# Loading the expert stage's tables and weights in 1 MB pieces, four slots in flight instead of two of 2 MB

## The chip, the core and the metric

The kernel runs on one core of a Trainium2 chip. The core has TensorE (PE in the profile; PEld is its weight load), VectorE (DVE), ScalarE (ACT), GpSimd (POOL) and SyncE (SP), each with its own instruction stream, 16 DMA engines that they share. Of the tiles named below, `bank` is PSUM and all others are SBUF. All data is float32. The metric is the device time of one execution in microseconds (us); lower is better.

## The reference

One inference step of a two-layer backbone over 640 tokens (128 context, 512 latent; five blocks of 128) of width 1024. Each layer has a mixer (retention and Fourier mixing in layer 0, a convolution module in layer 1) and then the expert stage that this change is about. Every sub-layer is shifted, scaled and gated by rows that come from the conditioning vectors through a 1024 x 6144 matrix per layer (`ada_w`). The expert stage, cut to what is computed:

```
q = (x @ w_q).reshape(T, PEER_HEADS, 2, PEER_DQH)
scores = jnp.einsum('thsd,hskd->thsk', q, sub_keys)
s, i = lax.top_k(scores, PEER_TOPK)
cand = s[:, :, 0, :, None] + s[:, :, 1, None, :]          # 16 x 16 sums per head
cidx = i[:, :, 0, :, None] * PEER_NKEYS + i[:, :, 1, None, :]
top, sel = lax.top_k(cand, PEER_TOPK)
idx = jnp.take_along_axis(cidx, sel, axis=-1)             # 8 heads x 16 experts of 16384
g = jax.nn.softmax(top, axis=-1)
a = jax.nn.gelu(jnp.einsum('td,thkd->thk', xb, u_tab[ib]))
out = jnp.einsum('thk,thkd->td', g * a, v_tab[ib])
```

`w_q` is 1024 x 2048, and `u_tab` and `v_tab` have 16384 rows of 1024, 64 MB each per layer.

## The kernel before

The expert stage (`peer` in each engine's block) splits the tokens. For the first two blocks (GB = 2) the chosen rows are gathered: GpSimd issues 256 indirect DMAs of u rows and 256 of v rows per layer, 512 KB each, into rings of four, and VectorE does one dot product instruction per u gather (`dot`, L1336) and one multiply-add per v gather (`add`, L1354). For the other three blocks (DB = 3, 384 tokens) all 16384 experts are computed on TensorE: the tables are streamed from HBM, the activations of all experts are taken with gelu, and a dense gate matrix, zero where an expert was not chosen, is multiplied in.

The stage has two halves. In the **first half** TensorE works through jobs. `peer_jobs` (L375) lists them: 16 `q` jobs (128 columns of w_q against 640 tokens), 128 `u` jobs (128 experts against 384 tokens; 4 of them are a chunk of the table), and, in layer 0 only, 12 `ada` jobs (512 columns of layer 1's `ada_w` against the two conditioning vectors), one behind every second u chunk. Each job ends in one ScalarE instruction (`take_job`, L1009) that empties its bank of PSUM, and `job(n)` (L700) starts only when job n-2 is taken. The jobs' operands come in loads of 2 MB: four q jobs, four u jobs or one ada job share one. There are two slots, `load_slot` (L221), and SyncE (`peer_weights`, L486) issues load n into the slot of load n-2 when the last job of load n-2 is done. Between these it writes the finished activations of a chunk (768 KB, `acts`, L498) and the ada row (4 KB, `mod_rows`, L501) to HBM, and before it can write either, it waits until ScalarE has taken the job. SyncE's queue is in order. ScalarE's take of ada row i waits until the write of row i-1 has landed (`ada2_out`), since both use the same 512 columns of `ada_raw`.

Between the jobs TensorE also does the scores of the queries against the keys (`score`, L721; 40 per layer), which VectorE turns into the top 16 (`choose`, L1255), and, when all picks are made, 96 scatters per layer (`scatter`, L742) that make the dense gates out of one-hot rows which VectorE writes (`hot`, L1357, L1366 and L1368). VectorE's order is written out by `dve_order` (L393): dots and adds alternate at a steady pace with the choose, batch and hot steps between them. The stretch with the hot steps is called the **hot part** below, and what lies ahead of it in the first half the **choosing part**. `peer_steps_of` (L423) is a planner: it estimates when VectorE will want each score and scatter and puts them between the jobs by a table of costs, `COST = {"q": 8.9, "u": 5.4, "ada": 7.1}` us. ScalarE follows the same list.

The **second half** starts when the last job is taken, the last scatter is taken and the gates have been written to HBM. It streams v_tab, gates and activations through other slots and ends the stage. Of it the change touches only that two of its three v slots are described without `load_slot`; they are the same bytes.

Of the kernel before, what the change touches and what calls it, by code (L numbers as in the profile page):

```python
# [9 lines left out]
ALU = mybir.AluOpType  # L10
# [116 lines left out]
def program(nc, x_in, cond_t, norm_gain, final_gain, ada_w, ada_b, ada_fix_in, ab_w_in, ab_w_out, decays, states,  # L127
# [3 lines left out]
    with ctx:  # L131
# [89 lines left out]
        load_slot = [ring[:, i * 4096:(i + 1) * 4096] for i in range(2)]  # L221
# [9 lines left out]
        v_slot = [t.rearrange("p (j d) -> p j d", j=CT) for t in (work[:, 5120:9216], *load_slot)]  # L231
# [70 lines left out]
        load_in = per_stage("load_in", 2)  # L302
# [3 lines left out]
        top_ready = per_stage("top_ready", LAYERS); exp_ready = per_stage("exp_ready", LAYERS)  # L306
        idx_ready = per_stage("idx_ready", LAYERS)
        ijg_ready = sem("ijg_ready"); oh_ready = per_stage("oh_ready", LAYERS)
# [3 lines left out]
        gelu_ready = per_stage("gelu_ready", LAYERS)  # L312
# [4 lines left out]
        v_done = per_stage("v_done", LAYERS); d_sums = per_stage("d_sums", LAYERS)  # L317
# [12 lines left out]
        def chunk(parts, s, done, after=None):  # L330
# [7 lines left out]
                for c in range(8)]  # L338
# [6 lines left out]
                       ((u_free[0], ROWS), (v_free[0], ROWS), (d_sums[0], DB), (d_sums[0], DB))[c]) for c in range(4)]  # L345
# [29 lines left out]
        def peer_jobs(l):  # L375

            loads, jobs = [], []
            for c in range(CHUNKS):
                if c in (0, 2, 6, 10):
                    q = (0, 2, 6, 10).index(c)  # L380
                    loads.append(("q", q, len(jobs) + 4))
                    jobs += [("q", 4 * q + i, len(loads) - 1) for i in range(4)]
                loads.append(("u", c, len(jobs) + CT))
                jobs += [("u", c * CT + i, len(loads) - 1) for i in range(CT)]
                if l == 0 and c % 2 and c // 2 < ADA:
                    loads.append(("ada", c // 2, len(jobs) + 1))
                    jobs.append(("ada", c // 2, len(loads) - 1))
            return loads, jobs
# [32 lines left out]
        COST = {"q": 8.9, "u": 5.4, "ada": 7.1}  # L421
# [42 lines left out]
        load_base = [(0, 0), tuple(16 * ((len(plans[0][0]) + 1 - i) // 2) for i in range(2))]  # L464
# [19 lines left out]
        def _(sp):  # L484

            def peer_weights(l):  # L486
# [3 lines left out]
                for n in range(len(loads) + 2):  # L490
                    if n < 2:
                        sp.wait_ge(*first[n])
                    else:
                        kind, i, end = loads[n - 2]
# [7 lines left out]
                    if n == len(loads) or n == len(loads) + 1:  # L502
                        continue
# [1167 lines left out]
```

## Time and profile before

| | us |
|---|---|
| median of three runs | 4314.09 |
| lowest, highest | 4311.28, 4319.12 |
| the profiled execution, whole | 4313.75 |
| its span on the core | 4311.9 |
| mean granted TensorE clock | 0.965 of full speed |
| busy: PE / DVE / POOL / ACT | 4059.6 / 2616.0 / 1440.1 / 473.0 |
| moved by DMA | 1128.44 MB, 262 GB/s on average |

A row of the profile names a line of the kernel, an engine, an operation, and what it writes and reads (`ring<-in_peer_ut` is a load of the u table into the ring; `bank<-hT,ring` are the q and u jobs, `bank<-ring,stat` the ada jobs, `bank<-bc` the scatters; `bc` at L1366 and L1368 the hot steps). Idle time stands before the instruction that ended it, with the thing that released it. Many helper calls share one line: all matmuls are at L652, all ScalarE instructions at L952, so the names tell them apart. Of the mean granted clock, 1.0 is 2.4 GHz and 0.5 is 1.2 GHz. The DMA share is the mean busy share of the 16 DMA engines.

### The profile page before, as it was taken

To read this page: it belongs to the slowest core of one execution; us is meant where nothing else is said; L and a number is where in the kernel's file an instruction comes from. 1 tells how busy PE (TensorE), PEld (TensorE's weight loads), DVE (VectorE), ACT (ScalarE), POOL (GpSimd) and SP (SyncE) were. 2 spreads that over 40 slices of the span, in tenths; PEclk is the share of its full clock that TensorE was granted. 3 is DMA by queue.
4 is the path that set the end of the run, shared out by engine and by line. 5 is a ranking of instruction groups with operands and counts; after the bars stand their busy time and mean duration, and the time that the engine had idled before them with its cause. 6 is when DMAs were issued, how large, how long until landed. Compare 5 with 4: busy or idle time off the path is not lost.

```text
span 4311.9 us, 35262 instructions
## 1 busy us (share of the span) xinstructions
PE 4059.6 (94%) x12920; PEld 2247.2 (52%) x12920; DVE 2616.0 (61%) x5488; ACT 473.0 (11%) x879; POOL 1440.1 (33%) x1072
## 2 busy tenths in 40 slices
PE   8997899989999998999998999999999986999998
PEld 1655555555555663444444545666656664444443
DVE  2303577767767884433434954888887887443444
ACT  2010111101111220000001121111112221000000
POOL 0000014444445553333320000454555565333331
PEclk9998999999999998999999999999999986999999
DMA  8111247778889999888873100788889999888875
GB/s 318 60 58 62 93 171 288 282 269 314 313 314 348 355 343 374 318 331 322 316 281 123 59 30 20 280 313 298 328 330 342 353 330 321 356 328 321 321 304 184
DMA packets 349757, 1128.44 MB, mean 262 GB/s; under 512 B 23424, under 2 KB 139632, under 8 KB 328712
## 3 DMA queue, kind: packets, MB, share of 16 engines
q0 software_dynamic: 153632, 560.15, 35.2%
q1 hardware_dynamic: 96880, 515.69, 31.0%
q10 hardware_dynamic: 99072, 50.33, 3.9%
q8 instruction: 103, 1.69, 0.2%
q14 instruction: 70, 0.57, 0.0%
HBM read 1025.01 MB, written 101.07 MB: 261 GB/s over the span
## 4 chain that ended last, share of the span: by engine, by line
PE 88%; DMA 6%; DVE 5%; ACT 1%; issue 0%; SPq 0%; ACTq 0%; POOL 0%; DVEq 0%
PE bank L652 88%; DMA ring<-in_peer_ut 2%; DMA peer_gates<-work 2%; DMA ring<-in_peer_w_q 1%; DVE bc L1366 1%; DVE diag L1354 1%; DVE ring L1336 1%; DVE bc L1368 1%; DMA ring<-in_ada_w 1%; ACT work L952 0%; ACT hT L952 0%; DMA bc<-peer_gates 0%; DVE work L1190 0%; DVE work L1192 0%; PE bank L696 0%
## 5 line engine op out<-in xcount | busy, mean ns | idle before, releaser
L652 PE MATMUL bank<-hT,ring 128*128 128x384 f32 (+3 forms) x5696 | 1808.5, 477 | 59.5 <-DMA ring<-in_peer_ut 30.3
L652 PEld LDWEIGHTS bank<-hT,ring 128*128 128x128 f32 x5696 | 1062.0, 193 | 728.0 <-issue 89.2
L612 POOL DMA_INDIRECT ring<-in_peer_u,work x512 | 769.9, 1504 | 1728.4 <-DVE ring L1336 1456.6
L652 PE MATMUL bank<-ring,work 128*128 128x512 f32 x2016 | 868.8, 592 | 0.0
L612 POOL DMA_INDIRECT ring<-in_peer_v,work x512 | 644.5, 1259 | 302.1 <-issue 155.6
L1354 DVE SCALAR_TENSOR_TENSOR diag<-ring,work,diag 128x1024 f32<-128x1024 f32 x508 | 652.8, 1285 | 29.5 <-DMA ring<-in_peer_v,work 26.1
L1336 DVE SCALAR_TENSOR_TENSOR ring<-ring,work 128x1024 f32<-128x1024 f32 x512 | 622.2, 1215 | 22.7 <-DMA ring<-in_peer_u,work 22.7
L652 PEld LDWEIGHTS bank<-ring,work 128*128 128x128 f32 x2016 | 383.0, 190 | 482.2 <-issue 482.2
L1393 DVE TENSOR_TENSOR work<-work,bc 128x1536 f32<-128x1536 f32 x64 | 112.4, 1758 | 717.2 <-PE bank L652 666.0
L952 ACT ACTIVATE work<-bank 128x384 f32<-128x384 f32 (+3 forms) x540 | 290.7, 541 | 2029.8 <-PE bank L652 1928.6
L652 PE MATMUL bank<-work 128*128 128x512 f32 x1056 | 461.3, 597 | 30.8 <-DVE work L1393 30.8
L652 PE MATMUL bank<-ring,hT 128*128 128x384 f32 (+1 forms) x960 | 351.0, 524 | 8.5 <-ACT hT L952 8.5
L652 PEld LDWEIGHTS bank<-work 128*128 128x128 f32 x1056 | 202.2, 192 | 285.5 <-issue 285.5
L1366 DVE TENSOR_SCALAR bc<-keep,bc 128x128 f32<-128x128 f32 x768 | 214.0, 363 | 132.6 <-PE bank L652 82.8
L652 PE MATMUL bank<-bc 128*128 128x128 f32 x1536 | 225.1, 304 | 61.8 <-DVE bc L1368 58.6
L652 PEld LDWEIGHTS bank<-ring,hT 128*128 128x128 f32 x960 | 180.9, 191 | 162.4 <-issue 73.4
L652 PEld LDWEIGHTS bank<-bc 128*128 128x128 f32 x1536 | 215.0, 215 | 96.7 <-DVE bc L1368 67.1
L652 PE MATMUL bank<-ring,stat 128*2 128x512 f32 x384 | 168.5, 596 | 16.6 <-DMA ring<-in_ada_w 16.6
L1263 DVE MAX8 small<-bank 128x8 f32<-128x128 f32 x160 | 39.8, 290 | 222.6 <-PE bank L652 221.8
L1588 DVE SCALAR_TENSOR_TENSOR work<-work,small 128x670 f32<-128x670 f32 x180 | 149.5, 918 | 0.0
L952 ACT ACTIVATE work<-work 128x16 f32<-128x16 f32 (+3 forms) x49 | 14.1, 303 | 1164.1 <-DVE ring L1336 1151.2
L1368 DVE TENSOR_TENSOR bc<-bc,keep 128x512 f32<-128x512 f32 x192 | 132.1, 688 | 0.0
(156 smaller groups left out, 1595.1 us busy)
## 6 DMA issues: line engine op xcount, KB each, us to landing
ring<-in_peer_ut SPq DMA_DIRECT2D x64, 2048.0 KB
ring<-in_peer_vt SPq DMA_DIRECT2D x42, 2048.0 KB, 7.9
ring<-in_ada_w SPq DMA_DIRECT2D x24, 2048.0 KB, 14.4
peer_gates<-work ACTq DMA_DIRECT2D x48, 1024.0 KB
bc<-peer_gates SPq DMA_DIRECT2D x32, 1536.0 KB
peer_acts<-work SPq DMA_DIRECT2D x60, 768.0 KB
work<-peer_acts SPq DMA_DIRECT2D x60, 768.0 KB, 15.1
work<-in_peer_vt SPq DMA_DIRECT2D x22, 2048.0 KB, 7.9
```

The lines of the kernel that those rows point to most:

```text
L612: nc.gpsimd.indirect_dma_start(row, None, table, bass.IndirectOffsetOnAxis(ap=idx_all[:, i:i + 1], axis=0)).then_inc(s, 16)
L652: return nc.tensor.matmul(out, lhsT, rhs, start=start, stop=stop, **kw)
L952: return nc.scalar.activation(out, in_, func, **kw)
L1263: own.mark(v.max(side_v[:, s, 0:8], sc[s]))
L1336: v.scalar_tensor_tensor(out=row, in0=row, scalar=1.0, in1=h_tok[:, n % GB, :], op0=ALU.mult, op1=ALU.mult, accum_out=dots[:, n % 2, k:k + ...
L1354: v.scalar_tensor_tensor(out=a, in0=row, scalar=wgt[:, n % 2, k:k + 1], in1=a, op0=ALU.mult, op1=ALU.add).then_inc(v_free[l], 1)
L1366: v.tensor_scalar(oh[:, n % 2, 0, o, :], iota, ijg_t[:, 0, t0 + o:t0 + o + 1], ijg_t[:, 2, t0 + o:t0 + o + 1], ALU.is_equal, ALU.mult)
L1368: v.tensor_tensor(oh[:, n % 2, 1, :, :], ijg_t[:, 1, t0:t0 + OH].unsqueeze(2).to_broadcast([P, OH, NKEYS]), iota.unsqueeze(1).to_broadcast ...
L1393: v.tensor_tensor(w, a, g, ALU.mult).then_inc(w_ready[l], 1)
L1588: ins = v.scalar_tensor_tensor(out=y_conv[:, f, :], in0=src, scalar=w, in1=y_conv[:, f, :], op0=ALU.mult, op1=ALU.add)
```

## The change

The same bytes are loaded in pieces of half the size into four slots. A q load or a u load now feeds two jobs. An ada load is 256 columns, so one ada job becomes two of half the width: 24 jobs, 24 takes and 24 writes of 2 KB. Load n goes into the slot of load n-4 when that load's last job is done. The write of a u chunk stays whole, behind the second half of a chunk. Loads in layer 0: 96 instead of 48; in layer 1: 72 instead of 36. The rows of w_q and ada_w that a load reads are 1 KB long instead of 2 KB, those of u_tab 8 KB instead of 16 KB. The planner gets `"ada": 3.6` for the half job. Six pairs of per-layer semaphores (`top_ready`, `exp_ready`, `idx_ready`, `oh_ready`, `gelu_ready`, `d_sums`) become one counter each that goes on counting in layer 1.

```
-        load_slot = [ring[:, i * 4096:(i + 1) * 4096] for i in range(2)]
+        load_slot = [ring[:, i * 2048:(i + 1) * 2048] for i in range(4)]
...
+            def load_of(kind, c, n):
+                loads.append((kind, c, len(jobs) + n))
+                jobs.extend((kind, c * n + i, len(loads) - 1) for i in range(n))
+
             for c in range(CHUNKS):
-                if c in (0, 2, 6, 10):
-                    q = (0, 2, 6, 10).index(c)
-                    loads.append(("q", q, len(jobs) + 4))
-                    jobs += [("q", 4 * q + i, len(loads) - 1) for i in range(4)]
-                loads.append(("u", c, len(jobs) + CT))
-                jobs += [("u", c * CT + i, len(loads) - 1) for i in range(CT)]
+                for q in [n for n, at in enumerate((0, 0, 2, 2, 6, 6, 10, 10)) if at == c]:
+                    load_of("q", q, 2)
+                for half in range(2):
+                    load_of("u", 2 * c + half, 2)
                 if l == 0 and c % 2 and c // 2 < ADA:
-                    loads.append(("ada", c // 2, len(jobs) + 1))
-                    jobs.append(("ada", c // 2, len(loads) - 1))
+                    for half in range(2):
+                        load_of("ada", c // 2 * 2 + half, 1)
...
-        COST = {"q": 8.9, "u": 5.4, "ada": 7.1}
+        COST = {"q": 8.9, "u": 5.4, "ada": 3.6}
...
-                for n in range(len(loads) + 2):
-                    if n < 2:
-                        sp.wait_ge(*first[n])
+                for n in range(len(loads) + 4):
+                    if n < 4:
+                        if n % 2 == 0:
+                            sp.wait_ge(*first[n // 2])
                     else:
-                        kind, i, end = loads[n - 2]
+                        kind, i, end = loads[n - 4]
                         sp.wait_ge(jobs_done[l], end)
-                        if kind == "u" and i < CHUNKS - KEPT:
+                        if kind == "u" and i % 2 and i // 2 < CHUNKS - KEPT:
                             sp.wait_ge(job_taken[l], end)
-                            sp.dma_start(acts[l, i], a_stage[i % 2]).then_inc(a_out[i % 2], 16)
+                            sp.dma_start(acts[l, i // 2], a_stage[i // 2 % 2]).then_inc(a_out[i // 2 % 2], 16)
                         if kind == "ada":
                             sp.wait_ge(job_taken[l], end)
-                            sp.dma_start(mod_rows[1][:, i * CH:(i + 1) * CH], ada_raw).then_inc(ada2_out, 16)
...
+                            sp.dma_start(mod_rows[1][:, i * 256:(i + 1) * 256], ada_raw[:, 0:256]).then_inc(ada2_out, 16)
...
-                        pe.wait_ge(load_in[ld % 2], load_base[l][ld % 2] + 16 * (ld // 2 + 1))
+                        pe.wait_ge(load_in[ld % 4], load_base[l][ld % 4] + 16 * (ld // 4 + 1))
...
                     elif kind == "ada":
                         if i:
                             act.wait_ge(ada2_out, 16 * i)
-                        f(ada_raw, bank[0:2, 2 * (n % 2), :]).then_inc(job_taken[l], 1)
+                        f(ada_raw[:, 0:256], bank[0:2, 2 * (n % 2), 0:256]).then_inc(job_taken[l], 1)
```

Two places show what moves. The first is SyncE's queue in layer 0, from the load of the second ada piece to that of the third, at a point where no q load follows. `peer_acts<-work` writes a finished u chunk, `mod_rows<-work` an ada row. Before:

```order
L508 DMA ring<-in_ada_w 128x8x512
L498 DMA peer_acts<-work 128x1536 [waits job_taken0,jobs_done0]
L506 DMA ring<-in_peer_ut 128x4096
L501 DMA mod_rows<-work 2x512 [waits job_taken0,jobs_done0]
L506 DMA ring<-in_peer_ut 128x4096
L498 DMA peer_acts<-work 128x1536 [waits job_taken0,jobs_done0]
L508 DMA ring<-in_ada_w 128x8x512
```

And now:

```order
L512 DMA ring<-in_ada_w 128x8x256 [waits jobs_done0]
L502 DMA peer_acts<-work 128x1536 [waits job_taken0,jobs_done0]
L512 DMA ring<-in_ada_w 128x8x256
L510 DMA ring<-in_peer_ut 128x2048 [waits jobs_done0]
L502 DMA peer_acts<-work 128x1536 [waits job_taken0,jobs_done0]
L510 DMA ring<-in_peer_ut 128x2048
L505 DMA mod_rows<-work 2x256 [waits job_taken0,jobs_done0]
L510 DMA ring<-in_peer_ut 128x2048
L505 DMA mod_rows<-work 2x256 [waits job_taken0,jobs_done0]
L510 DMA ring<-in_peer_ut 128x2048
L512 DMA ring<-in_ada_w 128x8x256 [waits jobs_done0]
```

Before, the u load that TensorE needs right behind the ada job is issued behind the write of the u chunk just ahead of that job. Now the first half of that table chunk stands two jobs earlier, ahead of the write, and only its second half stands behind it. There are two writes of ada rows, each with its own wait for ScalarE.

The second place is ScalarE's queue in layer 0 around the fourth and fifth ada rows; 128x384 are the takes of u jobs, 128x640 of q jobs, `small<-small 128x80` is the exponential of the softmax for which VectorE waits. Before:

```order
L952 ACTIVATE work<-bank 2x512 [waits ada2_out,jobs_done0]
L952 ACTIVATE work<-bank 128x384 [waits a_out0,jobs_done0]
L952 ACTIVATE work<-bank 128x384 [waits jobs_done0] x3
L952 ACTIVATE work<-bank 128x384 [waits a_out1,jobs_done0]
L952 ACTIVATE work<-bank 128x384 [waits jobs_done0] x3
L952 ACTIVATE work<-bank 2x512 [waits ada2_out,jobs_done0]
L952 ACT_TABLE_LOAD
L952 ACTIVATE small<-small 128x80 [waits top_ready0]
L952 ACTIVATE work<-bank 128x640 [waits scores0,jobs_done0] x4
```

And now:

```order
L956 ACTIVATE work<-bank 2x256 [waits ada2_out,jobs_done0] x2
L956 ACTIVATE work<-bank 128x384 [waits a_out0,jobs_done0]
L956 ACTIVATE work<-bank 128x384 [waits jobs_done0] x3
L956 ACTIVATE work<-bank 128x384 [waits a_out1,jobs_done0]
L956 ACTIVATE work<-bank 128x384 [waits jobs_done0] x3
L956 ACTIVATE work<-bank 2x256 [waits ada2_out,jobs_done0]
L956 ACT_TABLE_LOAD
L956 ACTIVATE small<-small 128x80 [waits top_ready]
L956 ACTIVATE work<-bank 2x256 [waits ada2_out,jobs_done0]
L956 ACTIVATE work<-bank 128x640 [waits scores0,jobs_done0] x4
```

Each take of an ada row waits for the write of the row before it. Before, eight takes of u jobs (and more) lie between two of them; now every second one stands directly behind the take whose write it waits for, or with the exponential between them.

## Rows read from the trace of the kernel before

**Rows 1.** The page, chain that ended last, by engine.
```profile
PE 88%; DMA 6%; DVE 5%; ACT 1%; issue 0%; SPq 0%; ACTq 0%; POOL 0%; DVEq 0%
```

**Rows 2.** Waits of PE, layer 0, choosing part: total us, times, longest.
```profile
PE bank L652 <- DMA ring<-in_peer_ut: 26.0, 6, 5.4
PE bank L652 <- DMA ring<-in_peer_w_q: 25.9, 3, 10.5
```

**Rows 3.** PE by form, layer 0 choosing part: count, busy, mean ns, idle before.
```profile
L652 PE MATMUL bank<-hT,ring 128*128 128x384 f32 x1153 | 389.5, 499 | 26.0 <-DMA ring<-in_peer_ut 26.0
L652 PE MATMUL bank<-hT,ring 128*128 128x320 f32 x384 | 110.6, 449 | 25.9 <-DMA ring<-in_peer_w_q 25.9
```

**Rows 4.** The same of layer 1, choosing part.
```profile
L652 PE MATMUL bank<-hT,ring 128*128 128x384 f32 x1344 | 438.4, 486 | 0.0
L652 PE MATMUL bank<-hT,ring 128*128 128x320 f32 x384 | 105.0, 432 | 0.0
```

**Rows 5.** Timeline around the second ada job: start, us, engine, [idle].
```profile
704.88 0.49 ACT L952 ACTIVATE work<-bank 128x384 f32<-128x384 f32 x1 [4.67 <-PE bank L652]
705.22 7.03 PE L652 MATMUL bank<-ring,stat 128*2 128x512 f32 x16
705.45 0.33 SPq L498 DMA_DIRECT2D peer_acts<-work  x1
712.95 0.25 SPq L501 DMA_DIRECT2D mod_rows<-work  x1
717.90 8.41 PE L652 MATMUL bank<-hT,ring 128*128 128x384 f32 x16 [5.01 <-DMA ring<-in_peer_ut]
```

**Rows 6.** The chain that ended last, the same place: start, us, what.
```profile
705.82 12.04 DMA ring<-in_peer_ut
```

**Rows 7.** Windows, both parts, both layers; last columns clock, DMA share, GB/s.
```profile
599.60:1225.00 625.40, 573.48 (x1816) 327.55 (x1815) 472.54 (x1275) 70.00 (x121) 274.88 (x198) 0.96 0.79 291
2709.60:3261.00 551.40, 551.40 (x1863) 343.01 (x1863) 472.36 (x1277) 70.45 (x124) 275.65 (x198) 1.00 0.85 312
1225.00:1617.00 392.00, 372.45 (x1610) 245.24 (x1609) 321.15 (x690) 83.56 (x154) 213.58 (x138) 0.98 0.95 344
3261.00:3620.00 359.00, 312.48 (x1367) 225.23 (x1366) 319.22 (x688) 76.10 (x139) 218.08 (x138) 0.86 0.96 336
```

**Rows 8.** Waits of DVE, layer 0, choosing part.
```profile
DVE small L1263 <- PE bank L652: 103.9, 19, 17.3
DVE small L1320 <- ACT small L952: 31.3, 6, 9.2
```

**Rows 9.** Waits of DVE, layer 1, choosing part.
```profile
DVE small L1263 <- PE bank L652: 55.3, 16, 8.4
```

**Rows 10.** Waits of DVE, PE and ACT, layer 0, hot part.
```profile
DVE bc L1366 <- PE bank L652: 57.8, 29, 5.4
PE bank L652 <- DVE bc L1368: 12.6, 9, 3.3
PE bank L652 <- DMA ring<-in_peer_ut: 4.3, 3, 1.9
ACT work L952 <- DMA peer_gates<-work: 27.4, 8, 8.4
```

**Rows 11.** Waits of PE for DVE, layer 1, hot part.
```profile
PE bank L652 <- DVE bc L1368: 46.1, 24, 3.1
```

**Rows 12.** Timeline, end of layer 0's first half.
```profile
1616.32 0.69 DVE L1368 TENSOR_TENSOR bc<-bc,keep 128x512 f32<-128x512 f32 x1
1635.83 2.04 PE L652 MATMUL bank<-work 128*128 128x512 f32 x2 [16.62 <-DVE work L1393]
```

**Rows 13.** The page, DMA issues: KB each, median us to landing.
```profile
ring<-in_ab_w_in SPq DMA_DIRECT2D x1, 1024.0 KB, 5.4
ring<-in_ab_w_out SPq DMA_DIRECT2D x2, 2048.0 KB, 7.7
```

**Rows 14.** Window, layer 0, second half.
```profile
1636.00:2296.50 660.50, 660.50 (x1536) 292.16 (x1536) 279.43 (x308) 5.68 (x13) 219.43 (x181) 1.00 0.82 318
```

More of the change, by code:

```diff
@@ L230, in program @@
         acc = diagf.rearrange("p (b d) -> p b d", b=GB)
-        v_slot = [t.rearrange("p (j d) -> p j d", j=CT) for t in (work[:, 5120:9216], *load_slot)]
+        v_slot = [t.rearrange("p (j d) -> p j d", j=CT) for t in (work[:, 5120:9216], ring[:, 0:4096], ring[:, 4096:8192])]
         w_slot = [work[:, 9216 + i * CE:9216 + (i + 1) * CE] for i in range(3)]
@@ L344, in program @@
                         for i in range(2)], CIN[c], (glu_sums, 2 * c + 2),
-                       ((u_free[0], ROWS), (v_free[0], ROWS), (d_sums[0], DB), (d_sums[0], DB))[c]) for c in range(4)]
+                       ((u_free[0], ROWS), (v_free[0], ROWS), (d_sums, DB), (d_sums, DB))[c]) for c in range(4)]
         before_cin = cin_c[0]
@@ L463, in program @@
         plans = [(*peer_jobs(l), peer_steps_of(peer_jobs(l)[1])) for l in range(LAYERS)]
-        load_base = [(0, 0), tuple(16 * ((len(plans[0][0]) + 1 - i) // 2) for i in range(2))]
+        load_base = [(0, 0, 0, 0), tuple(16 * ((len(plans[0][0]) + 3 - i) // 4) for i in range(4))]
         v_base = [(0, 0, 0), tuple(16 * ((CHUNKS + 2 - i) // 3) for i in range(3))]
@@ L505, in peer_weights @@
                     if kind == "u":
[L506 removed]
+                        sp.dma_start(load_slot[n % 4], peer_ut[l, c // 2][:, c % 2 * 2048:(c % 2 + 1) * 2048]).then_inc(load_in[n % 4], 16)
                     else:
[L508 to L509 removed]
+                        sp.dma_start(load_slot[n % 4].rearrange("p (k n) -> p k n", k=KT),
+                                     tall(peer_w_q[l] if kind == "q" else ada_w[1], c * 256, 256)).then_inc(load_in[n % 4], 16)
             def peer_values(l):
@@ L744, in scatter @@
                     n = b * OHS + g
-                    pe.wait_ge(oh_ready[l], n + 1)
+                    pe.wait_ge(oh_ready, l * DB * OHS + n + 1)
                     if i >= 2:
@@ L789, in peer @@
                         if n == CHUNKS - 1:
-                            last.then_inc(d_sums[l], 1)
+                            last.then_inc(d_sums, 1)
                     if n < CHUNKS - 1:
@@ L1053, in peer @@
                     elif kind == "exp":
-                        act.wait_ge(top_ready[l], a + 1)
-                        f(top_e, top_e, ACT.Exp).then_inc(exp_ready[l], 1)
+                        act.wait_ge(top_ready, l * PHEADS + a + 1)
+                        f(top_e, top_e, ACT.Exp).then_inc(exp_ready, 1)
                     elif kind == "gelu":
                         act.wait_ge(u_free[l], (a + 1) * TOPK)
-                        f(act16[:, a % 2, :], dots[:, a % 2, :], ACT.Gelu_apprx_tanh).then_inc(gelu_ready[l], 1)
+                        f(act16[:, a % 2, :], dots[:, a % 2, :], ACT.Gelu_apprx_tanh).then_inc(gelu_ready, 1)
                     elif kind == "turn":
```

45 lines of the change are left out of this document (21 added, 24 removed).

## The prediction

> **What bounds the kernel now.** I read the views in this order. The chain that ended last gives the engine: 88% of the span is TensorE and 6% DMA [rows 1]. So time comes off only where TensorE works less or waits less. The waits of TensorE by stretch show where it waits for loads. In layer 0's choosing part it waits 9 times, 51.9 us, for the load of a u chunk or of w_q [rows 2]; in the hot part 3 times, 4.3 us [rows 10]. That is 12 waits, one for each ada job. In layer 1, which has no ada jobs, its q and u matmuls show no idle time ahead of them in the same part [rows 4]. The timeline tells why. A u chunk is done at 704.9, the ada job runs from 705.22 for 7.03 us, SyncE issues the write of the chunk at 705.45 and the load into the freed slot at 705.82, and TensorE goes on at 717.90, when that load lands, after 5.01 us without work [rows 5, 6]. One 7 us job is the only cover of a load that takes 12.04 us.
>
> A wait costs more than its idle time. Behind it the first 16 matmuls of a u job take 8.41 us [rows 5]. With 438.4 us for 1344 in layer 1, where the clock is 1.00, 16 take 5.2 us [rows 4, 7]. The granted clock of the whole choosing part is 0.96 in layer 0 [rows 7]: some matmuls ran at 1.2 GHz after a wait. Over the part this is 389.5 us for 1153 matmuls against 0.326 us each, 13.4 us, and 110.6 against 105.0 us for the 384 of the q jobs, 5.6 us [rows 3, 4]. Together 19.0 us.
>
> **Does VectorE let TensorE run ahead?** The two are coupled: VectorE waits for scores, TensorE for one-hot rows. The comparison of the layers decides it. VectorE's work in the choosing part is the same, 472.5 and 472.4 us, in 625.4 and 551.4 us [rows 7]. So it idles 152.9 us in layer 0 and 79.0 us in layer 1. It waits 103.9 us for scores in layer 0 and 55.3 us in layer 1 [rows 8, 9], and 31.3 us more in layer 0 for the exponential, whose place in ScalarE's queue is behind takes of TensorE's jobs [rows 8]. VectorE thus waits for a late TensorE, and a TensorE without stalls takes it along.
>
> **The change, part by part.** *Load waits, choosing part.* A u job is 5.2 us. The first half of the table chunk behind the ada jobs is now issued two u jobs earlier, so it has 10.4 + 7.0 = 17.4 us. The second half is issued where the whole one was, but needed 10.4 us later, again 17.4 us. Ahead of the second half stands the write of 768 KB. Before, write and load, 2816 KB, took from 705.45 to 717.90, 12.45 us or 226 KB a us [rows 5]. 1792 KB then take 7.9 us, and at half that pace 15.9 us, still inside the cover. I cost the 12 waits at nothing afterwards. TensorE's own sum for the choosing part is 625.4 - 51.9 - 19.0 = 554.5 us. VectorE's is 472.5 + 79.0 = 551.5 us. The longer decides: -71 us. The bounds are 0 (VectorE does not follow) and -74 (VectorE's own idle time falls to layer 1's).
>
> *Hot part.* It lasts 392.0 us with 372.5 us of TensorE busy, 321.2 us of VectorE and a DMA share of 0.95, which is 372 us of work for the DMA engines [rows 7]. TensorE waits 4.3 us for loads and 12.6 us for VectorE, VectorE 57.8 us for TensorE, ScalarE 27.4 us for writes of gates [rows 10]. No single engine has slack above 20 us, so 0 to -20; I take -5, the load waits and a little clock. If TensorE arrives ahead of VectorE, more of its gain turns into waits like the 46.1 us of layer 1 [rows 11].
>
> *Halved ada jobs.* An ada matmul of 512 columns takes 7.03 / 16 = 0.44 us [rows 5], one of 384 takes 0.326 us, one of 320 takes 105.0 / 384 = 0.273 us [rows 4]: all near 0.86 ns a column. No row has 256 columns. In proportion two halves cost what one whole did. At the price of 384 columns they would cost 3.4 us more each time, 41 us in all; I go by the proportion and take +2 for 12 more job changes.
>
> *The ada writes.* The second take of a pair now waits until the write of the first has landed, and ScalarE's queue stands behind it. The first half job ends about 3.6 us after the u chunk, the write is issued 0.7 us after a job's end [rows 5], and 1792 KB are queued ahead of it from 0.6 us on. If it lands with them, that is at 8.5 us and the take ends at 9.1. TensorE needs that take when it starts the second u job behind, at 7.0 + 5.2 = 12.2 us. The cover is that u job, with 3 us to spare; if the write took as long as write and load do now, the take would end at 13.6, 1.4 us late, 17 us over 12 pairs. Bounds 0 and +17, I take +2. The exponentials that stand in ScalarE's queue behind a first or second take may come up to 2 us later for VectorE: +1.
>
> The Trainium skill (DMA: Bandwidth & Descriptors, Queues, rings and completion order) says that each DMA engine consumes a queue's descriptors in order and that the semaphore write lands only behind every earlier write of that engine. By it the write lands with the load ahead of it, which is how I count above; the trace has no landing time of this write. Without that rule the write would land sooner and the +2 would be 0.
>
> *Everything else.* SyncE issues 84 more loads at 0.33 to 0.43 us; its queue is waited for only through the loads, which have cover. Layer 1 has no load waits to lose in this stage, and its hot part waits for VectorE [rows 4, 11]: 0. The joined semaphores count the same events: 0. The second half of layer 0 is TensorE busy for 660.5 of 660.5 us [rows 14], and VectorE's dots and adds stand between steps that wait for it: it moves as a block, as does the stretch from the last hot step at 1616.32 to the first matmul of the second half at 1635.83 [rows 12].
>
> Sum: -71 - 5 + 2 + 2 + 1 = -71 us on the profiled execution's 4313.75, so 4243 us. The median of the runs is 4314.09, 0.3 us higher, which changes nothing.
>
> **The rivals.** (A) The forecast: 4243 us, its own range 4222 (hot part at -20) to 4262.
>
> (B) TensorE gains, but half of it comes back as waits for VectorE or for the DMA engines in the hot part, whose share is 0.95 already. For it: 46.1 us of such waits in layer 1 [rows 11]. Against: VectorE waits 57.8 us for TensorE in layer 0's hot part [rows 10]. 4314 - 71/2 = 4278 us.
>
> (C) The second take of an ada pair holds TensorE for 1.5 us each time, and 1.5 us more go to the clock behind it (a 5 us wait brought 3.2): 36 us over 12 pairs, 4279 us. The write would have to land at 13.1 us instead of 8.5. Against it stands the pace above.
>
> (D) Slower, by the same place. The write of 2 KB doesn't land with the 1792 KB ahead of it but needs, from its own issue, what a load needs now, 12.04 us [rows 6]. It is issued 4.3 us after the u chunk, so the take ends at 4.3 + 12.04 + 0.6 = 16.9 us, 4.7 us late, and behind such a wait TensorE loses another 3.2 us to the clock (8.41 against 5.2). 12 times 7.9 is 95 us, against 71 + 2 gained: 4336 us. It decides from a lateness of about 2.9 us on, that is a landing at 14.5 us or later. For it: ScalarE takes nothing else meanwhile, so TensorE stops whatever it has loaded. Against it: the write would need 10.2 us from its issue, while all that is queued ahead of it should land within 4.2.
>
> (E) A load of 1 MB keeps the DMA engines busier per byte. Alone on the queues, 1024 KB land in 5.4 us and 2048 KB in 7.7 us, 3.85 us per MB [rows 13]: 1.55 us more per MB. Layer 0's choosing part has 30 loads, 60 MB (1153 / 64 u loads, 384 / 128 q loads and 9 ada loads), its hot part 14 loads, 28 MB, layer 1's hot part 8 loads, 16 MB. The DMA engines' work is share times span [rows 7]. It becomes 494 + 93 = 587 us against 625, 372 + 43 = 415 against 392, and 345 + 25 = 370 against 359; layer 1's choosing part, 469 + 74 = 543 for 24 loads, stays under its 551. Sum -38 + 23 + 11 = -4: 4310 us, no change that can be told. Against it: both rows are single transfers, whose fixed end shows in full, while here up to three follow each other.
>
> The Trainium skill (DMA: Bandwidth & Descriptors, Bandwidth) speaks for E: it gives a 1 MB transfer 78% of the peak rate and 16 MB 97%. The fit on the same page, 2.0 us plus bytes at 436 KB a us, makes the extra 2.0 us per MB; by that, an estimate, the sum would be +57, about 4371 us. No row here has several 1 MB loads in flight at once in this stage.
>
> (F) The loads arrive late whatever the order, since the gathers take the bandwidth, and nothing changes: 4314 us. Against it: layer 1 moves 312 GB/s in the same part and has no load waits [rows 4, 7].
>
> **Chances.** A 0.68, B 0.14, C 0.08, D 0.04, E 0.03, F 0.03. Between 4305 and 4323 a measurement of this kernel can't tell a change from none (0.2%). Faster therefore 0.90 (A, B, C), same 0.06 (E, F), slower 0.04 (D). The range reaches from A's lower end to just above C, 4222 to 4282; D, E and F and a part of A's and C's outer ends, together under 0.2, are left out.
>
> **What would show it.** Waits of TensorE for loads in layer 0's first half near 0 (56.2 before), its granted clock in the choosing part near 1.00. The first hot step about 70 us earlier after the same first dot. VectorE's wait for scores near 55. Second half and layer 1 unchanged in length. Wrong would be: TensorE waits for ScalarE behind ada pairs (C, D), waits for `bc` in the hot part beyond 30 us (B), a DMA share at 1.00 with waits for loads (E).

## The result and the profile after

The changed kernel takes 4235.41 us (median of 4 runs, 4233.7 to 4239.63) against 4312.68 us for the kernel before, run beside it (4 runs): a ratio of 0.9822, 95% interval 0.9805 to 0.9839. That is 77 us, between 69 and 84, faster. The forecast was 4243 us, 71 us faster, in a range of 4222 to 4282. The profiled execution has a span of 4233.8 us, 78.1 us less than before. The lines that the rows name stand four lower in the changed kernel: the matmuls at L656 and no longer at L652, the dots at L1340, the hot steps at L1370 and L1372. The rest of a row reads as before.

The chain that ended last, by engine. The DMA share was 6% [rows 1]:

```profile
PE 91%; DVE 5%; DMA 3%; ACT 1%; issue 0%; ACTq 0%; POOL 0%; SPq 0%; DVEq 0%
```

No TensorE wait for a load is left in the expert stage; before there were 12, 56.2 us [rows 2, 10]. The windows of the same parts (layer 0's choosing part, layer 1's, layer 0's hot part, layer 1's, layer 0's second half; columns as in [rows 7]):

```profile
595.70:1154.50 558.80, 558.80 (x1973) 332.24 (x1972) 472.77 (x1277) 71.99 (x131) 274.77 (x198) 1.00 0.90 327
2630.20:3184.50 554.30, 554.30 (x1875) 344.99 (x1874) 472.06 (x1276) 71.04 (x125) 274.74 (x199) 1.00 0.86 311
1154.50:1538.50 384.00, 370.81 (x1659) 247.83 (x1657) 320.38 (x688) 84.24 (x158) 215.24 (x138) 0.99 0.97 349
3184.50:3543.40 358.90, 309.63 (x1370) 222.77 (x1369) 319.82 (x690) 76.34 (x139) 218.10 (x138) 0.88 0.96 337
1558.00:2218.00 660.00, 659.18 (x1532) 291.94 (x1533) 280.53 (x309) 5.68 (x13) 217.25 (x181) 1.00 0.82 319
```

Layer 0's choosing part went from 625.4 to 558.8 us, and TensorE is busy in all of it at a clock of 1.00. Its hot part went from 392.0 to 384.0 us. Layer 1's parts last 554.3 and 358.9 us after 551.4 and 359.0, and the second half 660.0 after 660.5 [rows 7, 14]. VectorE's work is what it was, 472.8 and 320.4 us. Counted between the same VectorE instructions (first dot, first hot step, last hot step), the times were 599.65, 1225.57 and 1616.32 us and are now 595.7, 1154.6 and 1537.8: 4 us of the gain lie ahead of the first dot, 67.1 in the choosing part, 7.5 in the hot part, 78.6 in all, and nothing of it is given back later.

TensorE's matmuls by form in layer 0's choosing part, which answer to [rows 3]:

```profile
L656 PE MATMUL bank<-hT,ring 128*128 128x384 f32 x1162 | 380.3, 486 | 0.0
L656 PE MATMUL bank<-hT,ring 128*128 128x320 f32 x384 | 105.2, 433 | 0.0
L656 PE MATMUL bank<-ring,stat 128*2 128x256 f32 x288 | 64.1, 379 | 0.0
```

The u and q matmuls cost 380.3 / 1162 = 0.327 and 105.2 / 384 = 0.274 us, layer 1's price of before [rows 4]: the matmuls at 1.2 GHz are gone with the waits. The halved ada jobs cost 64.1 us in the part.

Who waits for whom now in layer 0: the first two rows are of the choosing part, the next three of the hot part, the last, ScalarE's wait for the writes of ada rows, of both:

```profile
DVE small L1267 <- PE bank L656: 53.2, 17, 7.8
DVE small L1324 <- ACT small L956: 15.1, 3, 6.3
DVE bc L1370 <- PE bank L656: 52.9, 27, 4.8
PE bank L656 <- DVE bc L1372: 7.9, 6, 3.1
PE bank L656 <- ACT work L956: 5.3, 3, 2.8
ACT work L956 <- DMA mod_rows<-work: 46.7, 11, 6.3
```

VectorE's waits for scores fell from 103.9 to 53.2 us, those for the exponential from 31.3 to 15.1 [rows 8]. ScalarE waits 46.7 us for the writes of ada rows, 4.2 us each time, and TensorE waits 5.3 us for ScalarE in the hot part and not at all in the choosing part.

The timeline around the second ada pair, in the place of [rows 5], in order of time:

```profile
683.72 0.33 SPq L510 DMA_DIRECT2D ring<-in_peer_ut  x1
694.05 0.49 ACT L956 ACTIVATE work<-bank 128x384 f32<-128x384 f32 x1 [4.67 <-PE bank L656]
694.38 7.07 PE L656 MATMUL bank<-ring,stat 128*2 128x256 f32 x32
694.61 0.33 SPq L502 DMA_DIRECT2D peer_acts<-work  x1
694.98 0.43 SPq L510 DMA_DIRECT2D ring<-in_peer_ut  x1
698.03 0.37 ACT L956 ACTIVATE work<-bank 2x256 f32<-2x256 f32 x1 [3.50 <-PE bank L656]
698.48 0.25 SPq L505 DMA_DIRECT2D mod_rows<-work  x1
701.76 0.37 ACT L956 ACTIVATE work<-bank 2x256 f32<-2x256 f32 x1 [3.36 <-DMA mod_rows<-work]
701.93 3.39 PE L656 MATMUL bank<-hT,ring 128*128 128x384 f32 x10
```

The chunk is taken at 694.05. The first piece of the next chunk was issued at 683.72, 18.2 us ahead of its use at 701.93, and needs nothing more. The write of the first ada half is issued at 698.48 and ScalarE can take the second at 701.76, so it landed 3.3 us after its issue. The two half jobs, 16 matmul instructions each, take 7.07 us together, after 7.03 for the whole job.

### The profile page after: what moved, and what is told of

Same layout as the page of the kernel before. It is cut to its first block, busy times and chain, and to the rows that moved or that the text cites. A ratio compares the mean times of both kernels' runs of the same rounds, so it can differ in the third digit from the quotient of the medians.

```text
span 4233.8 us, 35864 instructions
## 1 busy us (share of the span) xinstructions
PE 4036.7 (95%) x13112; PEld 2248.0 (53%) x13112; DVE 2615.7 (62%) x5488; ACT 475.2 (11%) x891; POOL 1439.5 (34%) x1072
## 4 chain that ended last, share of the span: by engine, by line
PE 91%; DVE 5%; DMA 3%; ACT 1%; issue 0%; ACTq 0%; POOL 0%; SPq 0%; DVEq 0%
PE bank L656 91%; DMA peer_gates<-work 2%; DVE bc L1370 1%; DVE diag L1358 1%; DVE ring L1340 1%; DVE bc L1372 1%; DMA ring<-in_ada_w 1%; ACT work L956 0%; ACT hT L956 0%; DMA bc<-peer_gates 0%; DVE work L1194 0%; DVE work L1196 0%; PE bank L700 0%; DVE x L1409 0%; PE bank L819 0%
## 5 line engine op out<-in xcount | busy, mean ns | idle before, releaser
L656 PE MATMUL bank<-hT,ring 128*128 128x384 f32 (+3 forms) x5696 | 1790.4, 473 | 3.3 <-ACT hT L956 3.3
L656 PEld LDWEIGHTS bank<-hT,ring 128*128 128x128 f32 x5696 | 1052.7, 191 | 660.8 <-issue 77.3
L656 PE MATMUL bank<-ring,work 128*128 128x512 f32 x2016 | 868.8, 592 | 0.0
L656 PEld LDWEIGHTS bank<-ring,work 128*128 128x128 f32 x2016 | 383.0, 190 | 482.2 <-issue 482.2
L1340 DVE SCALAR_TENSOR_TENSOR ring<-ring,work 128x1024 f32<-128x1024 f32 x512 | 622.4, 1216 | 23.6 <-DMA ring<-in_peer_u,work 23.6
L956 ACT ACTIVATE work<-bank 128x384 f32<-128x384 f32 (+4 forms) x552 | 293.0, 534 | 1949.5 <-PE bank L656 1829.5
L656 PE MATMUL bank<-work 128*128 128x512 f32 x1056 | 460.2, 596 | 33.4 <-DVE work L1397 33.4
L656 PE MATMUL bank<-ring,hT 128*128 128x384 f32 (+1 forms) x960 | 351.2, 524 | 8.5 <-ACT hT L956 8.5
L656 PEld LDWEIGHTS bank<-work 128*128 128x128 f32 x1056 | 201.8, 191 | 287.4 <-issue 287.4
L1370 DVE TENSOR_SCALAR bc<-keep,bc 128x128 f32<-128x128 f32 x768 | 214.0, 364 | 124.6 <-PE bank L656 79.2
L656 PE MATMUL bank<-bc 128*128 128x128 f32 x1536 | 220.7, 300 | 62.5 <-DVE bc L1372 57.1
L656 PEld LDWEIGHTS bank<-ring,hT 128*128 128x128 f32 x960 | 180.8, 191 | 162.6 <-issue 73.6
L656 PEld LDWEIGHTS bank<-bc 128*128 128x128 f32 x1536 | 210.9, 212 | 96.8 <-DVE bc L1372 65.8
L656 PE MATMUL bank<-ring,stat 128*2 128x256 f32 (+1 forms) x576 | 171.4, 456 | 14.7 <-DMA ring<-in_ada_w 14.7
L1372 DVE TENSOR_TENSOR bc<-bc,keep 128x512 f32<-128x512 f32 x192 | 132.2, 688 | 0.0
## 6 DMA issues: line engine op xcount, KB each, us to landing
peer_gates<-work ACTq DMA_DIRECT2D x48, 1024.0 KB, 10.3
```

What stands on the lines that cost most here:

```text
L656: return nc.tensor.matmul(out, lhsT, rhs, start=start, stop=stop, **kw)
L956: return nc.scalar.activation(out, in_, func, **kw)
L1340: v.scalar_tensor_tensor(out=row, in0=row, scalar=1.0, in1=h_tok[:, n % GB, :], op0=ALU.mult, op1=ALU.mult, accum_out=dots[:, n % 2, k:k + ...
L1370: v.tensor_scalar(oh[:, n % 2, 0, o, :], iota, ijg_t[:, 0, t0 + o:t0 + o + 1], ijg_t[:, 2, t0 + o:t0 + o + 1], ALU.is_equal, ALU.mult)
L1372: v.tensor_tensor(oh[:, n % 2, 1, :, :], ijg_t[:, 1, t0:t0 + OH].unsqueeze(2).to_broadcast([P, OH, NKEYS]), iota.unsqueeze(1).to_broadcast ...
```

## The experiments

Each ran beside the kernel before, on the same chip, and is given as a ratio to it. e1 to e4 shared one chip, e5 to e8 a second, e9 to e11 a third; e12 ran on a fourth. The *cover* of a load is the work that TensorE has between the issue of the load and its first use. Code is cut to what matters; `...` marks a cut.

**e1, the mark.** The changed kernel again. 

> The changed kernel once more, as the mark for the three kernels beside it. All theories: 4235 us within 5 us, a ratio to before of 0.982.

Measured: 4234.37 us (5 runs), 0.9820 (0.9805 to 0.9834). Its choosing part lasts 558.8 us, as in the first profile.

**e7, no loads of ada_w.** The kernel before; what is left out is said in the expectation. The ada job counts to the load of the u chunk ahead of it, and the ada row is written together with that chunk.

```
-                loads.append(("u", c, len(jobs) + CT))
+                ada = l == 0 and c % 2 and c // 2 < ADA
+                loads.append(("u", c, len(jobs) + CT + bool(ada)))
...
-                    loads.append(("ada", c // 2, len(jobs) + 1))
```

> The kernel before without the 12 loads of ada_w in layer 0; the ada jobs, takes and writes stay, and multiply what lies in the slot of the u chunk ahead (this leaves out layer 1's true modulation rows). Theory 'the 7 us ada job as the only cover of a 2 MB load is the whole cause': no waits for loads in layer 0, choosing part about 559 us as in the changed kernel, 4230 to 4240 us. Rival 'the DMA engines' bandwidth is what TensorE waits for': the 24 MB less give more than the change did, below 4220 us. Rival 'loads of 2 MB cost something besides': above 4250 us.

Measured: 4227.25 us, 0.9812 (0.9795 to 0.9828). The windows of layer 0's two parts:

```profile
595.20:1149.90 554.70, 554.70 (x1817) 318.30 (x1817) 472.70 (x1278) 70.07 (x121) 274.87 (x198) 1.00 0.81 295
1149.90:1529.60 379.70, 367.08 (x1605) 242.19 (x1604) 319.56 (x687) 83.67 (x154) 213.39 (x138) 0.99 0.94 337
```

With slots and loads of 2 MB, and only the ada loads gone, TensorE has no waits for loads, and the choosing part takes 554.7 us. The prediction's sum for TensorE alone was 554.5 us. This run takes out both the place of the ada load in the two slots and its 24 MB. The bytes are not what counted: the changed kernel moves all of them and has no waits either, and its median is only 7 us above this one, of which 4 are in the choosing part; the intervals of the two ratios overlap. 4227 us is 3 us under the range that I gave and above the 4220 of the bandwidth rival. What is left is the place of the ada load in the slots.

**e5, two slots of 1 MB.** The changed kernel with `% 2` and `n - 2` in the place of `% 4` and `n - 4`.

```
-        load_slot = [ring[:, i * 2048:(i + 1) * 2048] for i in range(4)]
+        load_slot = [ring[:, i * 2048:(i + 1) * 2048] for i in range(2)]
```

> The changed kernel with two slots of 1 MB: the smaller pieces without the longer reach. Theory 'cover decides': the second ada half is then issued behind the write of the chunk and has 3.5 us of cover; it lands 8.5 to 11 us behind the chunk's end, so TensorE waits 5 to 7.5 us at each of 12 pairs, 60 to 90 us, and some 3 us each time go to the clock: 4330 to 4365 us, slower than before. Between chunks without ada jobs 10.4 us of cover are just enough. Rival 'smaller pieces are what helps': 4311 us or less.

Measured: 4356.66 us, 1.0105 (1.0088 to 1.0123), inside the range of the cover theory. TensorE's waits for loads in layer 0's first half, and the window of the choosing part:

```profile
PE bank L656 <- DMA ring<-in_ada_w: 85.2, 13, 11.9
PE bank L656 <- DMA ring<-in_peer_w_q: 7.3, 3, 5.3
PE bank L656 <- DMA ring<-in_peer_ut: 1.1, 2, 0.6
592.60:1250.60 658.00, 583.33 (x1975) 338.40 (x1974) 472.95 (x1278) 71.90 (x131) 275.32 (x199) 0.94 0.78 278
```

The waits moved to the ada loads, nearly all to the second half of a pair, 6.6 us each, and the granted clock of the part is 0.94. Small pieces without more slots lose 45 us.

**e4, three slots of 1 MB.** The same edit with 3. 

> The changed kernel with three slots of 1 MB instead of four: load n waits for load n-3. The first u piece behind an ada pair is then issued behind the write of the chunk, with the two half ada jobs, 7.0 us, as its cover. Theory 'cover decides': write and piece, 1792 KB at 226 KB a us, land 8.5 us behind the chunk's end, so TensorE waits about 1.5 us each time, 18 us over 12 pairs, hardly any of it lost to the clock: about 4253 us (4243 to 4265). Rival 'the smaller piece alone is enough': 4235 us. Rival 'the number of slots is what counts, cover or not': waits also between u chunks without ada jobs.

Measured: 4273.83 us, 0.9908 (0.9891 to 0.9924), outside the 4243 to 4265 that I gave. TensorE's waits for loads in the choosing part, and its window:

```profile
PE bank L656 <- DMA ring<-in_peer_ut: 14.8, 5, 6.3
PE bank L656 <- DMA ring<-in_peer_w_q: 14.0, 3, 7.5
593.00:1189.00 596.00, 567.23 (x1973) 336.46 (x1972) 473.15 (x1278) 72.01 (x131) 274.77 (x198) 0.98 0.85 307
```

The mechanism holds and the price was too low. TensorE waits 8 times in the choosing part, where 9 pairs are, but 3.6 us each (up to 7.5 in front of q loads) and not 1.5, and 28.8 us of waits lengthened the part by 596.0 - 558.8 = 37.2 us.

**e6, the load ahead of the write.** The kernel before, with SyncE's two DMAs exchanged:

```
+                    if n < len(loads):
+                        ... sp.dma_start(load_slot[n % 2], ...)
                     if n >= 2:
+                        kind, i, end = loads[n - 2]
                         if kind == "u" and i < CHUNKS - KEPT:
                             sp.wait_ge(job_taken[l], end)
                             sp.dma_start(acts[l, i], a_stage[i % 2]).then_inc(a_out[i % 2], 16)
...
```

The same load behind the writes is taken out.

> The kernel before, two slots of 2 MB, but SyncE issues each load ahead of the write of the finished chunk (and of the ada row), not behind it. Theory 'cover against landing time': 2048 KB instead of 2816 KB must land, 3.4 us less at 226 KB a us, and the load is issued 0.35 us sooner; so each of the 12 waits of 4.7 us shrinks to about 1.3 us. 41 us off the waits and half of the 19 us of the clock: about 4262 us (4250 to 4275). Rival 'the place in SyncE's queue does not matter, since the DMA engines serve both at once': 4311 us.

Measured: 4311.63 us (10 runs), 1.0002 (0.9991 to 1.0012). The size that I expected is refuted, and the rival, for which the place in SyncE's queue does not matter, has the time right. Two loads in the chain that ended last, then waits of TensorE in the choosing part, its wait for ScalarE in the hot part and ScalarE's for the writes of gates, then both windows:

```profile
694.07 11.08 DMA ring<-in_peer_ut
842.98 11.22 DMA ring<-in_peer_ut
PE bank L652 <- DMA ring<-in_peer_ut: 22.5, 6, 5.0
PE bank L652 <- DMA ring<-in_peer_w_q: 18.3, 3, 8.7
PE bank L652 <- ACT work L952: 11.3, 3, 5.4
ACT work L952 <- DMA peer_gates<-work: 42.6, 8, 10.4
596.10:1211.00 614.90, 574.11 (x1815) 328.30 (x1814) 473.14 (x1278) 69.98 (x121) 274.84 (x198) 0.96 0.81 296
1211.00:1608.00 397.00, 373.63 (x1605) 246.78 (x1604) 319.81 (x687) 83.11 (x154) 212.44 (x138) 0.98 0.95 338
```

The first of these loads takes 11.1 us from its issue, where the load at the same place took 12.04 behind the write [rows 6]. But 12.04 was the longest of its kind. The chain holds six u loads of the choosing part in each profile: 10.4 to 11.9 us, 11.2 in the mean, here, and 8.9 to 12.0, 10.8 in the mean, before. So a write of 768 KB ahead of a u load cost it nothing that shows, not 3.4 us; the three q loads took 13.4 us in the mean after 15.0. What e6 gives the u loads is the issue 0.9 us sooner, since the load no longer stands behind ScalarE's take and the write (704.88 to 705.82 in [rows 5, 6]).

The waits for loads in the choosing part shrank by 11 us, to 40.8. In the hot part something comes back: TensorE waits 11.3 us for ScalarE, where it waited 2.7 in the profile before, and ScalarE waits 42.6 us for the writes of gates after 27.4 [rows 10]. That the exchange caused this is not shown, and single profiles don't settle it. e8 has the same layer 0 as the kernel before and shows 619.1 us for the choosing part against 625.9, and this hot part, 397.1 us, is 6 us longer than before's, but e9's is as long with before's instructions and a wait for ScalarE of 3.1 us. What the 10 runs say stands: no change.

**e9, more work where TensorE waits.** The kernel before with

```
+                        for k in range(6 if i < 9 else 0):
+                            mm(bank[0:2, 2 * (n % 2), :], cond[:, k, :], wide_w[:, k, :], k == 0, k == 5)
                         for k in range(KT):
```

> The kernel before with more work for TensorE where it waits: in the 9 ada jobs of layer 0's choosing part the first 6 of the 8 products are computed once more ahead of the job (its result is the same), 5.3 us each, 47 us in all. Theory 'a wait costs more than its idle time, by the clock': the filler stands in the place of waits of 4.3 us (u) and 8.6 us (q), of the q waits some 10 us are left, and the granted clock of the part goes to 0.99 or 1.00: choosing part 555 + 47 + 10 = 612 us, less than the 619 to 626 us of the kernel before; about 4303 us. Rival 'the 19 us are not the clock's after a wait' (busy DMA engines or memory slow the matmuls): they stay, 631 us, about 4320 us.

Measured: 4303.58 us (11 runs), 0.9986 (0.9977 to 0.9995). The profiled execution took 4311.37 us, one of the slowest of the 11. TensorE's waits for loads in the choosing part, and both windows:

```profile
PE bank L652 <- DMA ring<-in_peer_w_q: 12.4, 3, 6.8
PE bank L652 <- DMA ring<-in_peer_ut: 0.6, 1, 0.6
598.80:1218.00 619.20, 606.17 (x1925) 330.20 (x1924) 472.80 (x1278) 70.05 (x121) 274.93 (x198) 0.99 0.81 294
1218.00:1615.00 397.00, 375.77 (x1605) 246.52 (x1604) 319.72 (x687) 83.69 (x154) 213.00 (x138) 0.97 0.94 338
```

TensorE does 47 us more and the kernel is 6 us faster. Without the filler, waits of 51.9 us went with 19 us that the lower clock cost; with it 13.0 us of waits are left, and the clock's part is 619.2 - 554.7 - 47.5 - 13.0 = 4.0 us. The choosing part is longer than the 612 us of the expectation by these two. The DMA share is 0.81 after 0.79, so busy DMA engines are not what slowed the matmuls before: the clock's term belongs to the waits.

**e8, layer 1 alone.** Slots and pieces by layer, `NS = (2, 4)`, with layer 0 as before.

```
-        load_slot = [ring[:, i * 2048:(i + 1) * 2048] for i in range(4)]
+        NS = (2, 4)
+        load_slot = [[ring[:, i * 8192 // k:(i + 1) * 8192 // k] for i in range(k)] for k in NS]
```

> The change in layer 1 alone; layer 0 keeps two slots of 2 MB and whole ada jobs. Theory 'the change pays only at the ada jobs': 4311 us within 5 us, layer 0's choosing part at 626 us. Rival 'shorter loads help wherever the DMA engines are busy': 4300 us or less, out of layer 1's two parts (552 and 359 us).

Measured: 4312.19 us (10 runs), 1.0005 (0.9996 to 1.0015): no change, as expected. The choosing parts of layer 0 and layer 1:

```profile
598.10:1217.20 619.10, 570.03 (x1817) 325.85 (x1816) 473.05 (x1277) 70.05 (x121) 274.88 (x198) 0.96 0.80 294
2701.00:3256.00 555.00, 555.00 (x1877) 345.39 (x1876) 472.65 (x1278) 71.04 (x125) 275.07 (x199) 1.00 0.86 311
```

In layer 1 the part is 555.0 us, 3.6 longer, and nothing is lost by it: the first dot comes 3.3 us sooner, since the wait of VectorE for its first gather falls from 7.9 to 4.6 us in the changed kernel, while the end stays where TensorE puts it.

**e3, each load as two DMAs.** The changed kernel, 168 more DMAs (96 + 72; the figure of 336 in the expectation is all of them).

```
+                        for e in range(2):
+                            sp.dma_start(load_slot[n % 4][:, e * 1024:(e + 1) * 1024],
+                                         peer_ut[l, c // 2][:, c % 2 * 2048 + e * 1024:...]).then_inc(load_in[n % 4], 16)
```

> The changed kernel with each load of 1 MB issued as two DMAs of 512 KB into the same slot, 336 more DMAs in all. Theory 'cover decides, size does not': 4235 us within 5 us, no waits of TensorE for loads in layer 0's first half. Rival E (a fixed cost of each transfer loads the DMA engines, 1.55 us per step as 5.4 and 7.7 us to landing have it): 60 more transfers in layer 0's choosing part at 1.55 us are 93 us on 503 us of DMA work in 559 us, so waits for loads return and the time is above 4280 us.

Measured: 4237.14 us, 0.9824 (0.9809 to 0.9839), 3 us from e1 and within what can be told. Layer 0's parts:

```profile
590.50:1149.00 558.50, 558.50 (x1972) 332.18 (x1971) 472.74 (x1277) 71.90 (x131) 274.89 (x198) 1.00 0.91 327
1149.00:1534.00 385.00, 369.33 (x1656) 247.01 (x1656) 319.71 (x687) 83.70 (x157) 215.50 (x138) 0.99 0.97 347
```

558.5 us without a wait for a load, and DMA shares of 0.91 and 0.97 where the changed kernel has 0.90 and 0.97. Share times span is the DMA engines' work: 494 us before, 0.90 x 558.8 = 503 in the changed kernel, 0.91 x 558.5 = 508 here, where E had 587 for the changed kernel and 93 us more for this one. (The expectation even took E too low: by 5.4 and 7.7 us a transfer more costs 2 x 5.4 - 7.7 = 3.1 us, not 1.55.) Rival E is refuted. The Trainium skill (DMA: Bandwidth & Descriptors, Bandwidth) gives a transfer of 1 MB 78% of the peak rate and one of 16 MB 97%. No loss of that kind with smaller transfers shows here, where loads follow each other: neither 2 MB to 1 MB nor 1 MB to 512 KB brought waits for loads, and the second moved neither share nor time.

**e2, two places for the ada row.** The changed kernel with

```
-                        if i:
-                            act.wait_ge(ada2_out, 16 * i)
-                        f(ada_raw[:, 0:256], ...)
+                        if i >= 2:
+                            act.wait_ge(ada2_out[i % 2], 16 * (i // 2))
+                        f(ada_raw[:, i % 2 * 256:(i % 2 + 1) * 256], ...)
```

> The changed kernel with two places for the ada row in turn, so that the second take of a pair waits for the write of two rows ago and no longer for the one just issued. Theory 'the write waits are hidden' (the prediction's +2 and +1 us): ScalarE's waits for writes of ada rows, 46.7 us over 11 waits in the changed kernel, go to near 0, TensorE's few waits for ScalarE in the hot part (5.3 us) shrink, and the time falls by 0 to 5 us, to about 4232 us. Rival 'they are paid for' (C in small): the time falls by 10 us or more, and VectorE's waits for the exponential (15.1 us) fall with it.

Measured: 4233.05 us, 0.9817 (0.9798 to 0.9836), 1.3 us below e1. ScalarE's waits for the ada writes are gone from its list, and the parts last 559.0 and 377.7 us. The write waits were hidden, as predicted, within the few us that such runs differ by; C, at 36 us, and D are refuted.

**e10, e11, e12, the planner of layer 1.** Layer 1's hot part was bound by VectorE while VectorE idled for scores in its choosing part. On top of e2:

```
+            slower = 1.0 if any(kind == "ada" for kind, _, _ in jobs) else 1.08
...
-                now += COST[kind]
+                now += slower * COST[kind]
```

> The kernel with two ada rows (e2), and in layer 1 alone the planner counts every job 1.08 times as long, so that scores and scatters stand 3 to 10 jobs earlier in TensorE's order. Theory 'layer 1's first half ends with VectorE, and VectorE idles for scores that TensorE's order holds back': of its 58.5 us of waits for scores some 20 go, TensorE has 49 us of waits at the end to give: about 4213 us (4205 to 4222). Rival 'TensorE then waits for VectorE in the middle instead': 4233 us. Rival 'DMA engines at a share of 0.96 bound the hot part': a shorter choosing part and a longer hot part, 4230 us.

> As e10 with a factor of 1.2, scores up to 18 jobs earlier. Same theory: VectorE's waits for scores fall by 40 us or more, layer 1's first half is then bound by VectorE's own 792 us of work: about 4195 us (4185 to 4212), if TensorE's waits for VectorE stay small. Rival: TensorE stands waiting for scores to be read, its waits grow by as much as VectorE gains, 4225 us or more.

> As e10 with a factor of 1.12. At 1.08 layer 1's first half ended with VectorE (last job 3473, last scatter 3501 us), at 1.2 with TensorE's jobs (last scatter 3457, last job 3513). Theory 'the half is shortest where both end together': by interpolation both at about 3486 us, so 13 us less than e10: about 4180 us (4172 to 4190). Rival 'the writes and reads of the gates, or waits in the middle, take it': 4190 us or more.

Measured: 4192.76 us (0.9731, 0.9717 to 0.9744) at 1.08, 4211.69 us (0.9774, 0.9761 to 0.9787) at 1.2, and 4178.36 us (0.9699, 0.9684 to 0.9713) at 1.12. The first gave twice what I expected. The second came to the slow end of its range for a reason I had not named: TensorE's jobs came last there, at 3513 us, 57 behind the last scatter. The third was set between and landed on its forecast. It is faster than both kernels of this case, by 3.0% and 1.3%. Layer 1's first half in e12: waits of TensorE, two of VectorE, and the windows of choosing and hot part:

```profile
PE bank L658 <- DVE bc L1374: 14.8, 10, 3.1
DVE small L1269 <- PE bank L658: 8.1, 3, 4.6
DVE bc L1372 <- PE bank L658: 33.8, 22, 4.9
2631.50:3124.00 492.50, 488.54 (x1666) 305.57 (x1665) 472.31 (x1278) 64.65 (x112) 275.67 (x198) 1.00 0.91 330
3124.00:3485.70 361.70, 345.55 (x1543) 237.65 (x1542) 319.21 (x688) 80.56 (x150) 215.97 (x138) 0.99 0.98 355
```

The parts are 492.5 and 361.7 us, after 554.3 and 358.9 in the changed kernel; VectorE waits 8.1 us for scores where it waited 58.5, and TensorE's waits for one-hot rows fell from 49.3 to 14.8.

## Why the prediction was right

**The cause.** One 7 us ada job was the only cover of a load. Shown by the row of slots at one size of load, with the same bytes, over both parts of layer 0: four slots give no wait for loads, three 29.3 us, two 93.6 us; and by e7, which takes only the ada loads away (no wait, choosing part 554.7 us).

**The choosing part, -71.** Measured -67.1 from first dot to first hot step. The sum for TensorE, 554.5 us, is e7's 554.7 and, at 558.8, the changed kernel's but for 2.9 us by which the first dot now comes sooner (VectorE's first gather wait is 4.4 us after 7.3, and 7.3 in e7 too) and the halved ada jobs. From TensorE's first job to the first hot step it is 629.1 after 699.2 us, -70. Both of its terms are shown, the waits by the rows and the clock by e9.

**VectorE follows.** I took layer 1's idle time, 79.0 us, as what is left. It is 558.8 - 472.8 = 86.0, and the scores' part of it 53.2 against the 55 that I gave.

**The hot part, -5.** The term that was mis-sized. Between hot steps it was 383.2 us after 390.7 in the first profile, 7.5 shorter, and 378.1 and 377.4 us in e1 and e2, 12.6 and 13.3 shorter, inside the 0 to -20 of the bounds. TensorE is busy for 370.8 of 384.0 us; the DMA share went to 0.97 without harm.

**Halved jobs +2, ada writes +2, exponential +1.** 64.1 against 63.3 us is +0.8. I had counted the write of a row as landing with the load ahead of it, 8.5 us behind the end of the chunk. It had landed 7.7 us behind it, at 701.76 after 694.05, while the load ahead of it, issued at 694.98, took 8.3 us and landed at 703.3. So the write did not wait for the whole load, and the writes cost nothing that e2 could find. The Trainium skill (DMA: Bandwidth & Descriptors, Queues, rings and completion order) says that a semaphore write lands only behind every earlier write of the same DMA engine; what had landed engine by engine at 701.76, the trace does not show. The waits for the exponential halved instead of growing. So the +5 was nearly all too much, and with the hot part it makes the difference between -71 and -77. In the sum it had cancelled the -5 of the hot part; both were off to the same side.

**The rate behind the cover.** The step that failed, with no effect on the forecast: 226 KB a us for write and load together, read from a single load. By e6 a 2 MB load takes 10.8 us in the mean behind the write and 11.2 ahead of it. In e4 the five u loads of 1 MB that stand behind the write and are waited for took 8.1 to 12.9 us from their issue, 9.4 in the mean, so they landed 10.3 us behind the chunk's end and not at 8.5. The time to landing thus does not go by the bytes queued at one rate; what it goes by is open. The cover of 17.4 us was wide enough to hold any of these (the u loads of the changed kernel landed 4.9 to 14.6 us after their issue up to the hot part); the same figure gave wrong sizes for e4 and e6.

**Rival E's second sum.** From the 2.0 us for each transfer in the fit that it cites from the Trainium skill (DMA: Bandwidth & Descriptors) the prediction makes 2.0 us more for each MB, and +57. But two loads of 1 MB in the place of one of 2 MB add one fixed time for 2 MB, 1.0 us for each MB. By that estimate the work in the choosing part is 494 + 60 = 554 us, under TensorE's 554.5, the hot parts of the two layers grow by 8 and 2 us, and the sum is -71 + 8 + 2 = -61, 4253 us, inside the range. The fit thus speaks far less for E than the prediction has it.

**Layer 1, second half: 0.** Shown by e8 and the windows.

## What to carry to other kernels

Count the cover of each load, not its bandwidth: with k slots in turn, a load has the jobs of the k - 1 loads ahead of it as its cover, so with two slots one short job can be all of it, and average shares don't show it. Count a wait of TensorE for loads, in a part that it bounds, at more than its length (1.2 to 1.5 times here, by the runs below), and look where the time of a part is set: a VectorE that idles early and bounds late asks for its inputs to be placed sooner, which was worth another 55 us here.

## What the runs showed of the hardware

The kernel before around its second ada job, in windows of their own: the ada job, then what follows the wait of 5.01 us.

```profile
705.20:712.20 7.00, 7.00 (x18) 1.30 (x17) 6.70 (x22) 0.17 (x1) 2.81 (x2) 1.00 0.96 357
717.90:721.00 3.10, 3.10 (x5) 1.85 (x6) 3.10 (x3) 0.00 (x0) 2.79 (x2) 0.50 1.02 433
724.00:727.00 3.00, 3.00 (x11) 1.80 (x10) 3.00 (x2) 0.49 (x1) 2.61 (x2) 1.00 1.01 412
```

The granted clock is 1.00 in the job, 0.50 behind the wait and 1.00 again from 724 us on, at a DMA share near 1 all the while. In e9, with the filler at this place, TensorE does not wait and the clock is 1.00 from 703 to 722 us. So a kernel with 47 us more matmul work was 6 us faster: the work kept TensorE at 2.4 GHz where an idle stretch had left it at 1.2.

From the first dot to the last hot step of layer 0, load waits of 29.3 us (e4) and 93.6 us (e5) lengthened the stretch by 39.7 and 116.1 us against the first profile of the changed kernel, and 56.2 us (before) by 82.2 us against e7. That is 1.2 to 1.5 us for each us of wait.

Splitting loads of 1 MB in two DMAs left DMA shares and time where they were. And a part with waits for loads differed from profile to profile, 619.1 and 625.9 us for the same instructions, while the part without them, counted between the same VectorE instructions, took 558.6 to 558.9 us in seven profiles of six kernels.
